# The mLSTM value and output-gate projections as seven products of halves, filled between the attention's pieces

## The reference

```python
(q, k_c, v_c, k_s, v_s, k_w, v_w, g_nsa, mq, mk, mv, mo, mi, mf, cu) = jnp.split(h @ w_in, points, axis=-1)
a_out = nsa_attention(q, k_c, v_c, k_s, v_s, k_w, v_w, g_nsa, ...)
hm = mlstm_chunkwise(mq.reshape(shp), mk.reshape(shp), mv.reshape(shp), mi + mlstm_i_bias, mf + mlstm_f_bias)
hm = (jax.nn.sigmoid(mo.astype(jnp.float32)) * hm.reshape(B, S, MLSTM_WIDTH)).astype(h.dtype)
x = x + jnp.concatenate([a_out, hm, c], axis=-1) @ w_out
```

## Time and profile before

| | |
|---|---|
| median of three executions | 1425.89 us |
| profiled execution, its own time | 1428.03 us |
| its span from first to last instruction | 1426.2 us |
| PE busy | 1205.7 us (85%) |
| DVE busy | 483.6 us (34%) |
| ACT busy | 255.3 us (18%) |
| POOL busy | 13.5 us (1%) |
| HBM read | 476.05 MB, 335 GB/s over the span |

### The profile page before, as it was taken

One profiled execution on the slowest core, in us unless ns is written; L12 is line 12 of the kernel. 1 busy time (PEld: TensorE's weight loads), 2 busy tenths in 40 slices (PEclk: granted clock), 3 DMA queues, 4 the chain that ended last, 5 costly groups with the idle time before them and its releaser, 6 DMA issues.

```text
span 1426.2 us, 17903 instructions
## 1 busy us (share of the span) xinstructions
PE 1205.7 (85%) x7431; PEld 708.9 (50%) x7431; DVE 483.6 (34%) x1001; ACT 255.3 (18%) x629; POOL 13.5 (1%) x82
## 2 busy tenths in 40 slices
PE   8999999999999998669689958768587695876977
PEld 7999999766568753123244314224142241422422
DVE  5398997663875431121110220111101111011123
ACT  2101111444600122011111101002020010201112
POOL 2000000000010000000000000000000000000000
PEclk9999999999999999889999989989899898998989
DMA  9958677431644899999999999999999999999995
GB/s 318 274 158 194 167 161 236 119 82 38 165 112 166 346 413 426 429 427 427 428 428 428 426 428 427 427 427 429 428 426 427 429 427 425 431 426 426 429 427 237
DMA packets 133362, 479.34 MB, mean 336 GB/s; under 512 B 47804, under 2 KB 105632, under 8 KB 107552
## 3 DMA queue, kind: packets, MB, share of 16 engines
q1 hardware_dynamic: 126816, 477.58, 85.9%
q10 hardware_dynamic: 6464, 0.58, 0.4%
HBM read 476.05 MB, written 2.10 MB: 335 GB/s over the span
## 4 chain that ended last, share of the span: by engine, by line
PE 52%; DMA 43%; ACTq 2%; DVE 1%; ACT 1%; issue 1%; DVEq 0%
DMA ring<-in_expert_w_up_dram 36%; PE PS L1127 13%; PE PS L1447 10%; DMA spare<-in_expert_w_up_dram 6%; PE PS L1269 5%; PE PS L1169 3%; PE PS L1434 3%; PE PS L1246 2%; PE PS L1638 2%; ACTq L1862 2%; PE PS L1425 1%; PE PS L1221 1%; PE PS L1119 1%; PE PS L1648 1%; PE PS L1188 1%; PE PS L1509 1%
## 5 line engine op out<-in xcount | busy, mean ns | idle before, releaser
L1447 PE MATMUL PS<-ring,XG 128*32 128x512 f32 x1296 | 222.2, 734 | 147.9 <-DMA ring<-in_expert_w_up_dram 107.3
L1447 PEld LDWEIGHTS PS<-ring,XG 128*32 128x32 f32 x1296 | 57.6, 131 | 274.9 <-issue 271.8
L3068 DVE TENSOR_TENSOR hTe<-PS,sg 128x128 f32<-128x128 f32 (+1 forms) x31 | 9.9, 320 | 349.3 <-ACT sg L2193 349.1
L2885 DVE TENSOR_TENSOR x<-PS,x 128x1024 f32<-128x1024 f32 x41 | 50.2, 1225 | 209.8 <-PE PS L1526 208.4
L2181 ACT ACTIVATE Hs<-PS 128x512 f32<-128x512 f32 x30 | 17.9, 597 | 463.1 <-PE PS L1447 349.8
L1434 PE MATMUL PS<-ring,XG 128*64 128x512 f32 x192 | 84.6, 594 | 18.0 <-DMA ring<-in_expert_w_up_dram 14.5
L1526 PE MATMUL PS<-Y,SW 128*128 128x512 f32 (+2 forms) x176 | 90.6, 627 | 1.5 <-ACT ro L2289 1.5
L1447 PE MATMUL PS<-spare,XG 128*32 128x512 f32 x208 | 66.0, 793 | 27.8 <-DMA ring<-in_expert_w_up_dram 27.8
L1436 PE MATMUL PS<-ring,XG 128*64 128x512 f32 x192 | 85.0, 595 | 0.0
L1425 PEld LDWEIGHTS PS<-sel,xn 128*128 128x128 f32 x640 | 75.3, 191 | 13.0 <-issue 12.7
L1425 PE MATMUL PS<-sel,xn 128*128 128x128 f32 x640 | 77.6, 280 | 1.4 <-DVE x L2885 1.4
(11 more groups left out here) (494 smaller groups left out, 1577.2 us busy)
## 6 DMA issues: line engine op xcount, KB each, us to landing
ring<-in_expert_w_up_dram SPq DMA_DIRECT2D x53, 2048.0 KB, 23.8
ring<-in_expert_w_gate_dram SPq DMA_DIRECT2D x53, 2048.0 KB, 26.9
ring<-in_expert_w_down_dram SPq DMA_DIRECT2D x51, 2048.0 KB, 27.1
ring<-in_w_in_dram SPq DMA_DIRECT2D x17, 2048.0 KB, 9.5
spare<-in_expert_w_gate_dram SPq DMA_DIRECT2D x9, 2048.0 KB, 26.2
spare<-in_expert_w_up_dram SPq DMA_DIRECT2D x8, 2048.0 KB, 23.9
spare<-in_expert_w_down_dram SPq DMA_DIRECT2D x8, 2048.0 KB, 27.3
ring<-in_w_in_dram SPq DMA_DIRECT2D x16, 512.0 KB, 7.3
```

Of the source, the lines that this page charges most:

```text
L1447: mm = pe.matmul(PS[r:r + 32, 0, :], gathered_rows(q, 4 * c + j)[:, column:column + 32], weight_rows(slots[u], 4 * (c % 2) + j), start=(c ...
L2885: dve.tensor_tensor(y, new, old, ALU.add).then_inc(sc_added, 1)
```

## The change

The four slabs `mv0`, `mv1`, `mo0`, `mo1` join `FAST_SLABS`. Their seven products are 56 matmuls of 128 columns for each slab, 224 in all, in the order m2, m1, m6, m7, m5, m3, m4, and are the fillers of the attention in place of the 128 matmuls of 256 columns. All seven results of a slab lie in PSUM banks 0 and 1, and the next slab uses the same places.

The four differences of each slab's weights are made by GpSimd (`late_left_sums`, `late_right_sums`, `late_end_sum`), each over 128 x 1024 elements with both inputs in SBUF; two of the four go to ring slot 2, which must be free for it, two overwrite quarters of the slab. DVE combines the seven results straight into `mv` and `mo` (`late_first`, `late_last`), and ACT's copies are gone. The token sums in `x1` live on through the attention, so the scores of steps 1 and 3 move from `x1` to ring slot 1. The fill counts of the attention change, and so do the slots into which the output projection's weights and the experts' weights are loaded; the third group of output weights now waits for the attention's last transpose, and the reload of `x1` comes ahead of it.

```diff
-OUT_SLOTS = [(1, 2), (3, 4), (0, 5), (1, 2)]
+OUT_SLOTS = [(3, 4), (5, 0), (1, 2), (3, 4)]
-TURN = [SPARE, 3, 4, 0, 5, 1, 2]
+TURN = [SPARE, 5, 0, 1, 2, 3, 4]
...
-              for tile in (att[:, :], x1[:, :, :].rearrange("p t d -> p (t d)"))]
+              for tile in (att[:, :], ring[:, 1, :, :].rearrange("p k n -> p (k n)"))]
...
+            def late_left_sums(i):
+                j, u = FAST_LATE + i, LATE_SLABS[i]
+                n = UNITS[u][0]
+                pool.wait_ge(w_loaded[n % RING], slab_at[n])
+                pool.wait_ge(unit_done, LATE if i < 2 else LATE_SLABS[i - 2] + 2)
+                pool.tensor_tensor(late_sums[:, i % 2, 0], quarter(u, 1, 1), quarter(u, 0, 1), ALU.subtract)\
+                    .then_inc(w_summed, 1)
+                pool.wait_ge(w_summed, 4 * j + 1)
+                pool.tensor_tensor(quarter(u, 0, 1), quarter(u, 0, 1), quarter(u, 0, 0), ALU.subtract)\
+                    .then_inc(w_summed, 1)
+            def late_right_sums(i):
+                pool.wait_ge(w_summed, 4 * j + 2)
+                pool.tensor_tensor(late_sums[:, i % 2, 1], quarter(u, 1, 1), quarter(u, 0, 1), ALU.subtract)\
+                    .then_inc(w_summed, 1)
+            def late_end_sum(i):
+                pool.wait_ge(prod_done, 2 * j + 1)
+                pool.wait_ge(w_summed, 4 * j + 3)
+                pool.tensor_tensor(quarter(u, 1, 0), quarter(u, 1, 0), late_sums[:, i % 2, 1], ALU.subtract)\
+                    .then_inc(w_summed, 1)
...
+                    if name == "m2":
+                        pe.wait_ge(first_scaled if i else unit_saved, SCALED + 2 * i - 1 if i else LATE - 2)
+                    if name == "m5":
+                        pe.wait_ge(first_scaled if i else unit_saved, SCALED + 2 * i if i else LATE)
+                    if name in ("m6", "m4"):
+                        pe.wait_ge(w_summed, 4 * j + {"m6": 3, "m4": 4}[name])
...
-            fill(8)
+            fill(16)
             pe.wait_ge(unit_saved, LATE)
             pe.wait_ge(cmp_saved, 1)
-            scores(0, 2)
+            scores(0, 5)
             scores(1, 3)
-            fill(16)
+            fill(32)
             pe.wait_ge(sT_ready, ML_H)
-            attend(0, 4)
-            scores(2, 3)
-            attend(1, 4)
+            attend(0, 7)
+            scores(2, 5)
+            fill(1)
+            attend(1, 7)
             mean_square(0)
-            scores(3, 3)
+            scores(3, 5)
             fill(LATE_STEPS)
...
+            def late_first(i):
+                dve.wait_ge(prod_done, 2 * (FAST_LATE + i) + 2)
+                step(dve.tensor_copy(late_a, late_part("m1")))
+                issued(dve.tensor_tensor(dst[:, 0, c:c + P], late_part("m2"), late_a, ALU.add))
+                step(dve.tensor_tensor(late_a, late_part("m6"), late_a, ALU.add))
+                dve.tensor_tensor(late_b, late_part("m7"), late_a, ALU.add).then_inc(first_scaled, 1)
+            def late_last(i):
+                dve.wait_ge(unit_done, u + 2)
+                dve.wait_ge(first_scaled, SCALED + 2 * i + 1)
+                both = issued(dve.tensor_tensor(late_a, late_part("m5"), late_a, ALU.add))
+                issued(dve.tensor_tensor(dst[:, 1, c:c + P], late_part("m4"), late_b, ALU.add))
+                issued(dve.tensor_tensor(dst[:, 1, c + P:c + 2 * P], late_part("m5"), late_b, ALU.add))
+                dve.wait_ge(dve_step, both)
+                dve.tensor_tensor(dst[:, 0, c + P:c + 2 * P], late_part("m3"), late_a, ALU.add).then_inc(first_scaled, 1)
             biases(0)
+            late_first(0)
+            late_last(0)
             biases(1)
             gated(0)
+            late_first(1)
+            late_last(1)
             gated(1)
+            late_first(2)
             biases(2)
+            late_last(2)
             head_squares(0)
             gated(2)
+            late_first(3)
             biases(3)
+            late_last(3)
             head_norm(0)
```

More of the change, by code:

```diff
@@ L219 @@
 LATE = units_before("mv")
+LATE_SLABS = [u for u in FAST if u >= LATE]
+FAST_LATE = len(FAST) - len(LATE_SLABS)
+LATE_PRODUCTS = ["m2", "m1", "m6", "m7", "m5", "m3", "m4"]
+LATE_STEPS = 8 * len(LATE_PRODUCTS) * len(LATE_SLABS)
+SCALED = 2 + FAST_LATE
+LATE_SAVED = SCALED + 2 * len(LATE_SLABS)
 HIDDEN_UNIT = units_before("w1v")
@@ L709, in _ @@
             for m, pair in enumerate(OUT_SLOTS):
-                if m < 3:
+                if m < 2:
                     sp.wait_ge(unit_done, max(last_use[s] for s in pair))
-                else:
-                    sp.wait_ge(p_turned, 2 * PAIRS_BY[-1])
+                elif m == 2:
                     for t in range(TT):
                         sp.dma_start(x1[:, t, :], x[0, t * P:(t + 1) * P, :]).then_inc(x_again, 16)
+                    sp.wait_ge(p_turned, 2 * PAIRS_BY[-1])
+                else:
                     sp.wait_ge(out_done, TT)
@@ L1162, in late_step @@
             def late_step():
-                u, k = LATE + late[0] // DK, late[0] % DK
-                n, part, kind, s, i = UNITS[u]
+                i, r = divmod(late[0], 8 * len(LATE_PRODUCTS))
+                name, k = LATE_PRODUCTS[r // 8], r % 8
+                j, u = FAST_LATE + i, LATE_SLABS[i]
+                n = UNITS[u][0]
                 if k == 0:
[L1167 to L1171, removed]
+                    if name == "m2":
+                        pe.wait_ge(w_loaded[n % RING], slab_at[n])
+                    if name == "m2":
+                        pe.wait_ge(first_scaled if i else unit_saved, SCALED + 2 * i - 1 if i else LATE - 2)
[3 more added lines that the diff above has]
+                        pe.wait_ge(w_summed, 4 * j + {"m6": 3, "m4": 4}[name])
+                tokens, weights = {"m1": (tok_11, quarter(u, 0, 0)), "m2": (tok_12, quarter(u, 1, 0)),
+                                   "m3": (tok_s4, quarter(u, 1, 1)), "m4": (tok_22, quarter(u, 1, 0)),
+                                   "m5": (tok_s1, quarter(u, 0, 1)), "m6": (tok_s2, late_sums[:, i % 2, 1]),
+                                   "m7": (tok_s3, late_sums[:, i % 2, 0])}[name]
+                mm = pe.matmul(late_part(name), tokens[:, k], weights[:, k], start=(k == 0), stop=(k == 7))
+                if k == 7 and name in ("m2", "m7"):
+                    mm.then_inc(prod_done, 1)
+                if k == 7 and name in ("m3", "m4"):
                     mm.then_inc(unit_done, 1)
@@ L1291, in _ @@
             pe.wait_ge(conv_out, CT)
-            pe.wait_ge(unit_saved, len(UNITS))
+            pe.wait_ge(first_scaled, LATE_SAVED)
             out_part(0, conv_f, True, False)
@@ L2042, in _, with exponents @@
                     pieces[name]()
-            late = [LATE]
-            def late_saves(n):
-                for u in range(late[0], late[0] + n):
-                    act.wait_ge(unit_done, u + 1)
-                    save_unit(u).then_inc(unit_saved, 1)
-                late[0] += n
-            def exponents(s, saves):
+            def exponents(s):
                 p, t = STEPS[s]
@@ L2064, in exponents @@
                     e.then_inc(exp_done, 1)
-                    if i == 1:
-                        late_saves(saves)
                 act.wait_ge(cmp_shifted, s + 1)
@@ L2085, in head_saves, with attend_saves @@
                                PS[:, 6 + s % 2, :].rearrange("d (i q) -> d i q", i=HPG), ACT.Copy).then_inc(o_saved, 1)
-            def attend_saves(s, saves):
+            def attend_saves(s):
                 for j in range(len(BLOCKS_OF[s])):
@@ L2091, in attend_saves @@
                         pieces["mlstm_root"]()
-                    if j == 3:
-                        late_saves(saves)
                 head_saves(s)
```

50 lines of the change are left out of this document (29 added, 21 removed).

## The result

| | kernel before | changed kernel |
|---|---|---|
| median | 1427.41 us (8 runs on the same chip) | 1430.93 us (8 runs) |
| profiled execution, its own time | 1428.03 us | 1431.22 us |
| span | 1426.2 us | 1429.1 us |
| POOL busy | 13.5 us | 53.3 us |

The ratio is 1.0029, with an interval from 1.0018 to 1.0040, and the medians are 3.5 us apart: the change costs time, where +0.35 us was forecast. (The forecast of 1426.2 us was counted from the 1425.89 us of three executions; eight give 1427.41.)

The account below looks back on a forecast made before the run. PE's work was taken to bound the kernel to about 550 us, then the experts' weights. Terms 2.4 + 0.0 - 2.8 + 0.75 = +0.35 us on the 1425.89 us median gave 1426.2 us, range 1423.0 to 1431.0.

Parts of the forecast that it names:

- The step that failed: Step 0's last score pair to attend(0)'s first transpose: DVE sets the pace, 26.37 us against 26.33 before, counted 0.0 us.
- The first stretch, +2.4 us,: First filler to step 0's last score pair: PE waits 1.1 us for GpSimd at m6; +2.4 us in all.
- the first rival: GpSimd's differences are slow, deciding from 3.1 us a pass; at 4.7 us a pass the time is 1433.6 us; chance 0.15.
- From attend(0) on: Shorter filler pieces save 2.8 us to step 3's scores; then late_last(3) ahead of head_norm(0) costs 0.75 us.
- the rivals of dearer and cheaper fillers: Narrow fillers between scores cost 4.8 us more (1431.0 us, chance 0.07) or 4.8 us less (1421.4 us, chance 0.12).
- DVE and GpSimd holding each other up: Rival: two-input DVE operations wait for GpSimd passes at the tails of steps 0 and 1; 1430.6 us, chance 0.04.
- The end follows the stage: A microsecond before 412.6 us moves the end by one; rival that it doesn't, time staying at 1425.9 us: chance 0.10.

Follow-up runs that it names:

- f1: Changed kernel with 20 added PE products that nothing reads, placed in its waits for GpSimd and DVE; 1427.84 us, ratio 1.0003.
- e1: Changed kernel with product m3 moved to third, ahead of the products needing GpSimd's differences; 1436.11 us, ratio 1.0056.
- e5: Changed kernel with m3 third and filler pieces of 8 and 4 in place of 7 and 5 in the attention; 1427.48 us, ratio 1.0003.
- e3: Changed kernel with m3 third, fillers 4 and 4 (not 5 and 3) in steps 0 and 1, late_last(0) after step 1's second head; 1433.61 us.
- e4: e3 with filler pieces of 8 and 4 in place of 7 and 5 in the attention; 1426.50 us, ratio 0.9996 to the kernel before.
- e2: Changed kernel with fillers 4 and 4 (not 5 and 3) in steps 0 and 1, late_last(0) after step 1's second head; 1428.74 us, ratio 1.0011.
- d3: Kernel before with three added GpSimd passes, PE waiting for the third behind the first score pair; 1426.09 us in one run.
- g: The changed kernel measured once more, unaltered; 1430.72 us, ratio 1.0029.

## Why the prediction was wrong

**The step that failed** is the one worked out as "Sum 26.37 us. **0.0 us.**", from step 0's last score pair to the first transpose of attend(0). It took 28.51 us. Its terms were right: DVE's eight operations take 2.04 us (288.83 to 290.87; 1.98 worked out), PE waits 2.01 us at the second slab's m2 ("some 2 us"), and a head takes 3.65 us where PE keeps up. What it lacked is that PE's wait isn't free even when DVE sets the pace: behind it the granted clock is at half, three fillers (six instructions) and a pair take 1.58 + 1.21 us where the forecast had 0.86 + 0.66, and PE becomes the slower of the two for two heads. In f1, with the clock held, the stretch takes 312.29 - 285.87 = 26.42 us, where 26.37 was forecast. So the fall is the whole error of this step, as far as one profile of each kernel shows it. No term of the forecast, no rival and no bound had the clock in it: it stood at 1.00 throughout, and I took that as a property of the stage, not of a stage in which PE hardly waits.

The Trainium skill has the mechanism in "TensorE: Matmul & The Clock Gate", Part 1: TensorE's clock is throttled when it is idle, and activity releases it; and the length of the slow stretch at a kernel's start changes from run to run. The rows agree with the first (2.01 us of idle time and a clock of 0.50 behind it, 1.00 with the idle time filled in f1), and show the second in the middle of a kernel too (e1 and e5, one program up to that place, with half clock to 294.0 and to 296.4 us). The forecast weighed neither.

**The first stretch, +2.4 us,** was mis-sized by 0.8 us. PE waits 1.90 us for GpSimd, not 1.1 (by the forecast's own times 271.5 - 270.47, which is 1.0): a pass takes 2.36 us in place of 2.17, each with 0.07 us behind it, and the first starts at 265.09 in place of 264.74, in part because the stage began 0.18 us later. Together (272.33 against 271.5) that is the 0.8 us. The rounds of a pair and a piece take 1.97 us as forecast. The mechanism of the first rival was at work, in small; its own bound of 3.1 us a pass was not reached. One of GpSimd's groups, answering to the earlier trace rows:

```profile
L899 POOL TENSOR_TENSOR ring<-ring 128x1024 f32<-128x1024 f32 x4 | 9.4, 2361 | 254.5 <-PE PS L1174 254.5
```

**From attend(0) on** the forecast held: -2.8 + 0.75 = -2.05 against -1.79 us. Pieces of 7 fillers take 1.76 to 1.78 us (1.75), of 5 1.31 (1.31), which ends the rivals of dearer and cheaper fillers, and the mean-square product waits 0.71 us for late_last(3), where 0.75 was forecast:

```profile
374.95 1.13 PE L1297 MATMUL PS<-hid,av_hd 128*128 128x512 f32 x2 [0.71 <-DVE hid L2701]
```

**What it adds up to.** Between the 3.76 us measured and the 0.35 forecast lie 3.41 us: 2.18 from the step that failed, 0.77 from GpSimd's wait, 0.26 from the stretch behind attend(0), 0.18 from a later start and 0.02 from the last stretch. That the median, 1430.93 us, still lies inside the range given, by 0.07 us, is luck: its top, 1431.0, is the time worked out for dearer fillers, and they were not dearer.

**DVE and GpSimd holding each other up** did happen, at two places off the path (below). **The end follows the stage,** within a scatter. In the changed kernel the products, the chain's first transfer and the median moved by 3.76, 3.77 and 3.5 us; in e1 the products moved by 8.0 us and the median by 8.7, in e3 by 6.3 and 6.2, in e4 by -0.8 and -1.0. But the products' start is that of one execution, and e2 (3.2 and 1.3 us), f1 (2.1 and 0.3) and e5 (2.8 and 0.0) agree less well. e5's profiled execution took 1430.78 us, 3.3 more than its median; that of d3 has its products 1.65 us later than the kernel before and ended 1.9 us earlier. The five waits of SP are there as before, 61.7 us in all.

**The loss, taken apart.** By the medians, f1 is 2.9 us under g, which is the clock. e4 is 1.3 us under f1: the waits themselves, together with e4's other pieces of fillers, which no run separates. And e4 stands 1.0 us under the kernel before, which its interval does not tell from nothing. By the start of the products, counted from the first filler of the same trace (before 146.69, after 150.27 in the first profile and 150.80 in g, f1 148.18, e4 145.97), the parts are 2.1 to 2.6, 2.2 and 0.7 us. The clock is the larger part by the medians alone; their intervals of about 1.3 us a side leave the split open. Open too is why a wait of 1.9 us lowers the clock in one execution and not in the next: behind GpSimd's it fell in g and in e2 and not in the changed kernel's first profile, behind DVE's 1.87 us in e2 and not in e3 and e4. Behind the longer ones, of 2.01 with 0.81 after a short piece, of 2.05, of 2.40 and of 2.53 us, it fell in every profile taken.

## What to carry to other kernels

Reckon that a new wait of PE can cost more than its length: waits of 2.40 us (where 0.45 stood) and of 2.53 us cost 3.6 and 4.0 us in the stage here, because PE came out of them at half clock. A wait of 2.01 us that lay within DVE's path, and was for that reason counted at nothing, cost 2.1 us. A granted clock of 1.00 in the trace of before holds for the waits it has, not for those that a change adds. Order the work so that what waits for a slow engine comes last and a product whose inputs are ready first, and check what that makes late next; cheap work in the gap keeps the clock where no order helps.

## What was unexpected of the hardware

Waits of about two microseconds were enough to halve PE's clock for 3 to 7 us in these traces. The twelve executions of g spread over 6.5 us and the eleven of f1 over 1.9; but the 23 of the kernel before beside them, whose trace has no such fall, spread over 5.3, so that the clock is not shown to make the spread.

One GpSimd pass took 4.37 us in place of 2.36. GpSimd's timeline, and DVE's at that time:

```profile
319.18 4.37 POOL L917 TENSOR_TENSOR ring<-ring 128x1024 f32<-128x1024 f32 x1 [12.99 <-PE PS L1228]
```

```profile
316.83 4.29 DVE L2690 TENSOR_SCALAR ring<-ring,rs 128x256 f32<-128x256 f32 x16
```

It is 2.0 us longer, about what DVE's run of scalings from SBUF to SBUF still had to go (to 321.12). It goes the other way too. A later run of sixteen (from 343.74 us, 128 columns) took 5.41 us, where the kernel before has 3.23, with a pass of GpSimd from 345.77 us on inside it. In e4 a run like the one at 316.83 took 12.90 us in place of 4.29: it began at 311.45, four passes of GpSimd followed each other from 311.72 on and kept their length (2.35 to 2.41 us), and DVE's scalings came late. Why the first pass got in there behind one scaling, and the one at 319.18 only behind the whole run, no run shows. The forecast had looked only at DVE operations that read two tiles. The Trainium skill, "SBUF — State Buffer", section "SBUF: two separate sides", counts DVE operations in a two-port mode among those that exclude GpSimd, for a whole instruction. Here the pass at 319.18 was held for the rest of a run, by 2.0 us; whether these scalings are in that mode no row shows. Nothing on the path waited in these places: no instruction of PE waited for that pass, and behind the long runs DVE stood idle for 7.97 us (changed kernel) and 2.58 us (e4) until PE had its next input.
